# Expert sums of a decoder layer: v rows gathered for each token, against one dense pass over the v table for two tiles at a time

## The reference, cut to what matters

```
q = (xb @ wq).reshape(tokens, 8 heads, 2, 128)
s = einsum('thpd,pkd->thpk', q, subkeys)          # two lists of 128 scores for each head
s1, i1 = top_k(s[:, :, 0], 16);  s2, i2 = top_k(s[:, :, 1], 16)
top_s, sel = top_k(s1[..., :, None] + s2[..., None, :], 16)   # 16 of 256 pairs
idx = (i1 * 128 + i2)[sel]                        # one of 16384 experts
g   = softmax(top_s)
act = gelu(einsum('thkd,td->thk', u_tab[idx], xb))
y   = einsum('thk,thkd->td', g * act, v_tab[idx])
```

## Time and profile before

| | us |
|---|---|
| runs | 2040.8, 2052.54, 2053.34 |
| median | 2052.54 |
| profiled execution, first to last instruction | 2046.0 |
| TensorE busy (share) | 1616.0 (79%) |
| VectorE busy | 1207.7 (59%) |
| ScalarE busy | 476.3 (23%) |
| GpSimd busy | 1134.0 (55%) |
| bytes moved | 713 MB, 349 GB/s over the span |
| of these by GpSimd's queue (the gathers) | 570 MB |

### The profile page before, as it was taken

The page is one execution under the profiler, slowest core; times in us unless marked ns, Lnnn a source line. Parts: engine busy times, 40 slices in busy tenths (PEclk is TensorE's granted clock), DMA queues, the critical chain, the costliest instruction groups (busy, mean ns, idle before and its releaser), DMA issues.

```text
span 2046.0 us, 20838 instructions
## 1 busy us (share of the span) xinstructions
PE 1616.0 (79%) x5461; PEld 764.0 (37%) x5461; DVE 1207.7 (59%) x3129; ACT 476.3 (23%) x1217; POOL 1134.0 (55%) x1168
## 2 busy tenths in 40 slices
PE   6979989983767457768888888788878789599966
PEld 1524546451126113223433344333433344255422
DVE  2222355867766701116767766677667689679972
ACT  1221313130101021212223222222222223223321
POOL 3000021322873555777777667767777677577773
PEclk8989999996775679998999989899999899899988
DMA  8795676896995599999999999999999999799995
GB/s 319 254 364 207 215 263 218 305 337 135 355 385 179 198 401 404 392 416 394 400 420 420 400 368 418 419 373 420 420 401 391 388 403 419 308 412 417 414 372 226
DMA packets 237575, 713.43 MB, mean 349 GB/s; under 512 B 23102, under 2 KB 49056, under 8 KB 237457
## 3 DMA queue, kind: packets, MB, share of 16 engines
q0 software_dynamic: 156672, 570.49, 71.2%
q1 hardware_dynamic: 80488, 140.73, 19.4%
q10 hardware_dynamic: 312, 1.07, 0.2%
HBM read 704.42 MB, written 8.25 MB: 348 GB/s over the span
## 4 chain that ended last, share of the span: by engine, by line
PE 19%; DMA 14%; DVE 12%; issue 7%; POOL 7%; ACT 5%; DVEq 0%; POOLq 0%; ACTq 0%
PE ps_y L2316 13%; DVE u_rows L2095 6%; DMA v_rows<-in_peer_v_dram,expert_idx_ring 5%; DMA v_rows<-in_peer_v_dram,tile_idx 5%; PE ps_r L2290 4%; POOL u_rows L1890 3%; DMA u_rows<-in_peer_u_dram,expert_idx_ring 3%; POOL v_rows L1896 2%; POOL v_rows L1904 2%; ACT wt_diag L1987 2%; PE ps_y L2331 2%; DMA v_rows<-in_peer_v_dram,sample_idx 1%; DVE key_scores_w L2106 1%; ACT L2002 1%; ACT L2033 1%
## 5 line engine op out<-in xcount | busy, mean ns | idle before, releaser
L2316 PE MATMUL ps_y<-v_rows,wt_diag 128*128 128x512 f32 x1664 | 796.9, 621 | 146.6 <-DMA v_rows<-in_peer_v_dram,expert_idx_ring 65.2
L2316 PEld LDWEIGHTS ps_y<-v_rows,wt_diag 128*128 128x128 f32 x1664 | 311.4, 197 | 571.1 <-issue 547.5
L1890 POOL DMA_INDIRECT u_rows<-in_peer_u_dram,expert_idx_ring x384 | 368.2, 959 | 164.7 <-issue 90.3
L2095 DVE CUSTOM_DVE_ANT_0 u_rows<-u_rows,ps_y 128x1024 f32<-128x1024 f32 x360 | 420.4, 1218 | 64.1 <-DMA u_rows<-in_peer_u_dram,expert_idx_ring 58.1
L1896 POOL DMA_INDIRECT v_rows<-in_peer_v_dram,expert_idx_ring x384 | 366.7, 955 | 120.2 <-issue 99.3
L341 POOL DMA_INDIRECT low_rows<-in_peer_u_dram,tile_idx x128 | 174.7, 1364 | 214.7 <-DVE tile_dots L333 148.5
L607 PE MATMUL ps_z<-w_stream,hT 128*128 128x512 f32 (+5 forms) x560 | 249.0, 602 | 36.9 <-DMA w_stream<-in_w_in_dram 19.7
L2331 PE MATMUL ps_y<-v_rows,wt_diag 64*64 64x512 f32 x1024 | 135.1, 645 | 57.4 <-DMA v_rows<-in_peer_v_dram,tile_idx 50.8
L333 DVE CUSTOM_DVE_ANT_0 low_rows<-low_rows,tile_rows 128x1024 f32<-128x1024 f32 x128 | 152.9, 1232 | 44.1 <-DMA low_rows<-in_peer_u_dram,tile_idx 31.9
L607 PEld LDWEIGHTS ps_z<-w_stream,hT 128*128 128x128 f32 (+1 forms) x560 | 100.9, 185 | 163.9 <-issue 132.6
L1904 POOL DMA_INDIRECT v_rows<-in_peer_v_dram,tile_idx x128 | 122.1, 954 | 71.8 <-PE ps_y L2331 44.6
(11 more groups left out here) (434 smaller groups left out, 1628.3 us busy)
## 6 DMA issues: line engine op xcount, KB each, us to landing
w_stream<-in_w_in_dram SPq DMA_DIRECT2D x25, 2048.0 KB, 12.8
w_stream<-in_ada_w_dram SPq DMA_DIRECT2D x12, 2048.0 KB, 12.8
w_stream<-in_peer_wq_dram SPq DMA_DIRECT2D x8, 1024.0 KB, 8.5
wq<-in_peer_wq_dram SPq DMA_DIRECT2D x4, 2048.0 KB, 42.2
w_stream<-in_w_in_dram SPq DMA_DIRECT2D x5, 1568.0 KB, 8.5
w_stream<-in_w_in_dram SPq DMA_DIRECT2D x5, 1536.0 KB, 17.5
u_rows<-in_peer_u_dram,expert_idx_ring POOLq DMA_INDIRECT x384, 7.4
v_rows<-in_peer_v_dram,expert_idx_ring POOLq DMA_INDIRECT x384, 7.9
```

Of the source, the lines that this page charges most:

```text
L1890: g.indirect_dma_start(u_rows[:, j, :], None, U, bass.IndirectOffsetOnAxis(where[:, j:j + 1], 0))\
L2095: v.tensor_tensor_reduce(u_rows[:, j, :], u_rows[:, j, :], row[:, :], 1.0, 0.0, ALU.mult, ALU.add, dots[:, par, j:j + 1]).then_inc(s["u_us ...
L2316: mm = nc.tensor.matmul(ps_y[:, c * 512:(c + 1) * 512], diag[:, par, j, :], v_rows[:, j, c * 512:(c + 1) * 512], start=(first and j == 0), ...
```

## The change

Routing is taken out of the loop over groups. q is made for all 416 remaining tokens at once, head by head; the scores of a head go to DRAM (`sc_dram`) and come back tile by tile. The work is then a list of 26 head steps `G`: 8 for each of tiles 2 to 4, and 2 for the samples, each with 16 u gathers and 16 dots.

The v gathers stay for tile 1 alone: 40 of them up front, the other 88 one to one with the u gathers of the first head steps. Its sums are now full 128x128 products. For tiles 2 to 4 and the samples the weights of all experts become dense matrices. Expert (a, b) is row a*128 + b of the table. For each token, VectorE compares the 128 selected a and b with 0..127 (`compare`), ScalarE scales one of the two one-hot matrices by the weights (`weigh`), and TensorE multiplies them (`build`), which gives the 128x128 matrix W of that token. Four tokens make a group; 32 groups a tile, 8 for the samples. W of two tiles fills the 16 MB of `expert_weights`.

Then the v table is streamed twice in 128 slabs of 128 rows (all a, one b), which SP loads with plain DMAs into rings: pass 1 serves tiles 2 and 3, pass 2 tile 4 and the samples (four slabs at a time, in four groups of 32 columns). W of tile 4 is built during the last 38 slabs of pass 1, that of the samples between the passes. The finish of tiles 1 to 3 is done in pass 2.

```
+DOT_GROUPS = {}
+for _n in range(TILE_GROUPS):
+    DOT_GROUPS.setdefault((NH - PH - 5) * TOPK + 2 * _n + 1, []).append(_n)
+    DOT_GROUPS.setdefault(2 * PH * TOPK + 6 + _n, []).append(TILE_GROUPS + _n)
+    DOT_GROUPS.setdefault(3 * PH * TOPK + 6 + _n, []).append(2 * TILE_GROUPS + _n)
...
 sync:
+                for n in range(2 * PK):
+                    dst, landed, _ = slab(n)
+                    m = n - PK
+                    if m < 0:
+                        if n >= 4:
+                            sp.wait_ge(s["passed"], n - 3)
+                    elif m < 4:
+                        sp.wait_ge(s["passed"], PK - 3 + m)
+                    elif m < 8:
+                        sp.wait_ge(s["u_used"], SLOTS)
+                    else:
+                        sp.wait_ge(s["passed"], PK + (m - 8) // 4 * 4 + 4)
+                    sp.dma_start(dst, I["peer_v"][0].rearrange("(a b) d -> a b d", b=PK)[:, n % PK, :]).then_inc(landed, 16)
 gpsimd:
+                def v0_gather(k):
+                    j = k % NB
+                    if k >= NB:
+                        pool.wait_ge(s["v_used"], k + 1 - NB)
+                    g.indirect_dma_start(v0_rows[:, j, :], None, V, ...)
...
+                for G in range(HEADS):
+                    pool.wait_ge(s["routed"], G + 1)
+                    if PH <= G + 2 < HEADS:
+                        load_scores(G + 2)
...
+                    first = V0_EARLY * NB + G * TOPK
+                    for r in range(TOPK):
+                        u_gather(G, r)
+                        if first + r < P:
+                            v0_gather(first + r)
 scalar:
+                def weigh(T, n):
+                    act.wait_ge(s["oh_cmp"], n + 1)
+                    for t in range(TG):
+                        col = (n - W_BASE[T]) * TG + t
+                        last = a(onehot[:, n % 2, 1, t, :], onehot[:, n % 2, 1, t, :], ACT.Copy, scale=tT[:, 0, col:col + 1])
+                    last.then_inc(s["oh_w"], 1)
 vector:
+                def compare(n):
+                    T = max(t for t in W_BASE if W_BASE[t] <= n)
+                    dve.wait_ge(s["w_out"], BANK_BASE[T] + 1)
+                    if n >= 2:
+                        dve.wait_ge(s["w_full"], bank_use(n - 2) + 1)
+                    t0 = (n - W_BASE[T]) * TG
+                    v.tensor_tensor(onehot[:, n % 2], iota[:, :].unsqueeze(1).unsqueeze(1).broadcast_to([P, 2, TG, PK]),
+                                    repeat_last(tT[:, 1:3, t0:t0 + TG], PK), ALU.is_equal).then_inc(s["oh_cmp"], 1)
...
+                for G in range(HEADS):
...
+                    for r in range(TOPK):
+                        take_dot(G, r)
+                        if r == 3 and G + 2 < HEADS:
+                            keys(G + 2)
+                        if r == 11 and G + 2 < HEADS:
+                            pairs(G + 2)
...
+                        for n in DOT_GROUPS.get(G * TOPK + r, ()):
+                            compare(n)
 tensor:
+                for h in range(PH):
+                    pe.wait_ge(wq_in[h // 2], 16)
+                    head(h)
+                    sums0(2 + h)
+                for i in range(2 + PH, TOPK):
+                    sums0(i)
+                columns_t(1)
+                for n in range(TILE_GROUPS):
+                    build(n)
+                columns_t(2)
+                for n in range(TILE_GROUPS, 2 * TILE_GROUPS):
+                    build(n)
+                pe.wait_ge(s["w_out"], BANK_BASE[2] + 1 + TILE_GROUPS)
+                pe.wait_ge(s["y_out"], 1)
+                for i2 in range(PK):
+                    products(i2, W[1][:, i2, :], 1)
+                    products(i2, W[2][:, i2, :], 2).then_inc(s["passed"], 1)
+                    if i2 == W3_FROM - 1:
+                        columns_t(3)
+                    if W3_FROM <= i2 < W3_FROM + TILE_GROUPS:
+                        build(2 * TILE_GROUPS + i2 - W3_FROM)
+                columns_t(ST)
+                for n in range(96, 96 + W_COUNT[ST]):
+                    build(n)
+                pe.wait_ge(s["w_out"], BANK_BASE[ST])
+                for i2 in range(PK):
+                    mm = products(PK + i2, region[:, i2 // HALF, i2 % HALF, :], 3)
+                    if i2 % 4 == 3:
...
+                        for c in range(2):
+                            for q in range(4):
+                                b = i2 - 3 + q
+                                mm = nc.tensor.matmul(y_banks[ST][c][q * NS:(q + 1) * NS, :], W[ST][:, b, :], ...)
+                        mm.then_inc(s["passed"], 4)
```

More of the change, by code:

```diff
@@ L2075, in _ @@
-                for k in range(2, GPT + 1):
-                    slot((LT - 1) * GPT + k, k % 2, pairs=LAST_PAIRS.get(k), keys=LAST_KEYS.get(k),
-                         squares=(LT, NS) if k == LAST_ROWS - 1 else None, rows=LT if k == LAST_ROWS else None)
-                y_copy(NG - 1)
-                group(NG + 1, 1)
-                root(NT - 1)
-                group(NG + 2, 0)
-                group(NG + 3, 1)
-                y_copy(NG + SG - 1)
-                root(NT, NS)
+                a(subT, bank[0][:, 0:2 * PK].rearrange("p (k n) -> p k n", k=2), ACT.Copy).then_inc(s["subT_out"], 1)
@@ L2182, in slot @@
-                def slot(i, par, gates, pairs=None, keys=None, before=None, rows=(h_ps, h_ps)):
-                    weigh(i, par, gates)
-                    if pairs is not None:
-                        route_pairs(*pairs)
-                    if before:
-                        before()
-                    take_dots(i + 1, 1 - par, range(0, NB // 2), rows[0])
-                    if keys is not None:
-                        route_keys(keys)
-                    take_dots(i + 1, 1 - par, range(NB // 2, NB), rows[1])
@@ L2194, in pair @@
-                def pair(i, first, H, p, before=None, rows=(h_ps, h_ps)):
-                    slot(i, 0, gate[:, bass.ds(first, NB)], keys=H, rows=rows)
-                    slot(i + 1, 1, gate[:, bass.ds(first + NB, NB)], pairs=(H, p + 2), before=before, rows=rows)
-                def finish(t, n, src, row):
-                    hold(dve, s["x1_in"], t * 16 + 16)
-                    chain(v.tensor_tensor(y[0:n, :], src, row, ALU.mult))
-                    chain(v.tensor_tensor(x1[0:n, :], x1[0:n, :], y[0:n, :], ALU.add))
-                    v.tensor_tensor_reduce(y[0:n, :], x1[0:n, :], x1[0:n, :], 1.0, 0.0, ALU.mult, ALU.add, fs[0:n, 0:1])\
-                        .then_inc(s["ss_ready"], 1)
-                    hold(dve, s["rt_ready"], t + 1)
+                    spread = iota[:, 0:TOPK].unsqueeze(1).unsqueeze(1).broadcast_to([P, 2, TOPK, TOPK])
@@ new lines, in finish @@
+                def finish(t, n, halves, row):
+                    dve.wait_ge(s["x1_in"], 16 * (NT + 2))
+                    x, y = x1[t][0:n, :], tmp[t % 2][0:n, :]
+                    for c, half in enumerate(halves):
+                        last = v.tensor_tensor(y[:, c * 512:(c + 1) * 512], half[0:n, :], row[0:n, c * 512:(c + 1) * 512], ALU.mult)
+                    chain(last)
+                    chain(v.tensor_tensor(x, x, y, ALU.add))
+                    v.tensor_tensor_reduce(y, x, x, 1.0, 0.0, ALU.mult, ALU.add, fs[0:n, 0:1]).then_inc(s["ss_ready"], 1)
+                    dve.wait_ge(s["rt_ready"], t + 1)
@@ L2244, in _ @@
-                chain.base, chain.n = outer + (LT - 1) * TILE, 0
-                def last_head(k):
-                    H = LAST_PAIRS.get(k)
-                    return None if H is None else (H, H if H < LT * PH else None)
-                def sample_norm():
-                    gained(NS, gain_s, 2 + 2 * B, 2)
-                    norm(LT, NS)
-                for k in range(2, GPT):
-                    first = (LT - 1) * P + k * NB
-                    last = k == GPT - 1
-                    if last:
-                        dve.wait_ge(s["hs_in"], 16 * QS)
-                        dve.wait_ge(spread_in[0], 2 * 16 * QS)
-                    slot((LT - 1) * GPT + k, k % 2, gate[:, first:first + NB], pairs=last_head(k), keys=LAST_KEYS.get(k),
-                         before=sample_norm if k == LAST_ROWS - 1 else None, rows=(h_smp, h_smp) if last else (h_ps, h_ps))
@@ L2277, in _, with sums0 @@
                 e = K["ident"]
-                def rows_t(t):
-                    hold(pe, s["h_normed"], t + 1)
+                def sums0(i):
+                    for j in range(NB):
+                        pe.wait_ge(s["diag_ready"], i * NB + j + 1)
+                        pe.wait_ge(v_in[j], i * 16 + 16)
+                        for c in range(2):
+                            mm = nc.tensor.matmul(bank[c][:, :], diag[:, i % 2, j, :], v0_rows[:, j, c * 512:(c + 1) * 512],
+                                                  start=(i == 0 and j == 0), stop=(i == TOPK - 1 and j == NB - 1))
+                        mm.then_inc(s["v_used"], 1)
```

877 lines of the change are left out of this document (436 added, 441 removed).

## The result

The changed kernel takes 2366.9 us (median of 4 runs, 2363.9 to 2374.0). The kernel before takes 2050.9 us on the same chip (4 runs, 2040.8 to 2053.3). The ratio is 1.155, with a 95% interval of 1.151 to 1.159: 316 us slower. The forecast was 2405 us, 353 us slower. The profiled execution took 2363.9 us and its span is 2362.2 us; against that span stands the sum of 2402.

A forecast was written before the change was run, and what follows sets the result against it. The prediction took DMA (1228 us of gathers) and GpSimd (1190 us) to bound the kernel before. The change's serial stages, added in order, gave 2402 us, 2408 against the run median, stated as 2405; range 2325 to 2520.

The forecast's parts named there:

- Step 1: From the start to the first routed head: head 0 at 781 us, routed at 816, first dot at 846.
- Step 2: Tile 2's u dots during tile 1's sums: 8 u gathers per 29 us, later 2.49 us a pair; sums end near 1130.
- Step 3: From 1141 us VectorE is the bound, 27.4 us a head without compares; W of tile 3 ready at about 1567.
- Step 4: First pass over the v slabs: 439 us of products, 46 builds, 2 waits, 20 for fighting gathers; end at 2074.
- Contention: In the first pass, slabs and gathers ask for 458 GB/s against 420, slowing some 35 slabs; taken as 20 us.
- Builds: In the first pass's last 38 slabs, 32 builds of four 128x128 products at 0.36 us each: 46 us.
- Step 5: Builds for the samples between the passes: 8 at ScalarE's 1.9 us plus 6 us to fill, 21 us, to 2095.
- Step 6: Second pass: 219 us of slab products plus 64 us of 32-column products on four column groups, 284 us, to 2379.
- the rival with 155 us more: In the second pass the 32-column products do not overlap: 219 us instead of 64, total 2560; chance 5%.
- the late slabs: In the second pass four slabs land together, every second group waits 3.9 us: 62 us, total 2467; chance 13%.
- Step 7: After the second pass: 11 us as before, plus 5 us for tile 4's finish ahead of the samples', to 2395.
- Step 8: TensorE's granted clock in the passes: 1% of 723 us, 7 us; at 0.94 it would be 45.

The follow-up runs named there:

- Experiment 2: The changed kernel with all eight heads made ahead of tile 1's sums 2 to 15: 2331.2 us, ratio 1.140 to the kernel before.
- Experiment 3: The changed kernel with each dot over 512 of the 1024 columns, gathers whole: 2285.3 us, one run.
- experiment 5: The changed kernel with both passes multiplying only columns 0 to 511 of each slab, slabs loaded whole: 2138.8 us, one run.
- Experiment 7: The changed kernel with the v table streamed three times, tile 2's pass starting once its own W is whole: 2395.2 us, ratio 1.166 to the kernel before.

## Why the prediction came true, step by step

In each step the measured time stands first.

- **Step 1, start.** First dot 840.8, predicted 846. The order of head, scores to DRAM and back, keys and pairs was worked from rows and each held.
- **Step 2, tile 2's dots.** Period 28.96 us against 29, tile 1's sums end at 1130 against 1130. Experiment 2 shows that the heads hold the u gathers, and that without the heads between the sums the DMA limit binds there; the gain is 35 us.
- **Step 3, VectorE.** From 1141 to 1564 it was busy 98%; first product at 1564.8 against 1567. GpSimd waits for dots in this stretch and not the other way round (its table of waits, 1141 to 1564, first row: who waited, for whom, us, times, longest). Experiment 3 shows it as cause: 79 us for half of the dots' columns.

```profile
POOL u_rows L1940 <- DVE tile_dots L2241: 103.2, 84, 6.9
```

- **Step 4, first pass.** 468.7 us against 507. The prediction had 439 + 46 + 2 + 20; the trace has 128 slabs of 3.44 us (440) and 28.5 of builds, with no waits. Two terms were mis-sized. **Contention** was put at 20 us and is 0: from 1564 to 1745 TensorE is busy 180.31 of 181 us at a DMA share of 1.02. The fight falls on the gathers: VectorE waits 25.2 us for u rows, and nothing on the chain waits for those dots. The row taken for it, the wq load at 4.3 us for 0.524 MB, was of another kind. Bytes by queue of the kernel before, 717 to 785 us, where q1 carries wq (packets, MB, share of the 16 engines):

```profile
q0 software_dynamic: 4570, 16.67, 60.4%
q1 hardware_dynamic: 5101, 10.96, 42.4%
```

  Of q1's 10.96 MB only 8.4 are wq; the rest is other loads of SP. So the queue as a whole moved 161 GB/s, where the prediction read 123, and 161 is already more than the 153 that the slabs ask for: read by queue, this row gives no contention. The packets are near even, but q1's hold 2.1 KB and the gathers' 3.6 KB, so q1 got 40% of the bytes. A slab's packets are as large as a gather's (3.6 KB in experiment 5), and there its even share is 205 GB/s. The Trainium skill (DMA: Bandwidth & Descriptors, "Queues, rings and completion order") says that each DMA engine goes round the queues that have work, a packet at a time. Its packet is a group of some 9 to 17 descriptors, while the profile counts 144 packets to a gather of 128 rows, so the turns themselves are not seen here. The near-even counts agree with the rule, and by it the term would have been 0. **Builds** were put at 46 us (0.36 us a 128x128 product) and took 28.5 (0.89 a build of four, which is 8 records). The row of 0.71 us for four records holds the latency of the last record, and in a run each record adds 0.11 us. A length in the timeline is no period; starts of neighbours are.
- **Step 5, sample builds.** 2033.5 to 2052.7, 19 us against 21.
- **Step 6, second pass.** 285.4 us against 284: four slabs in 7.06 + 1.85 = 8.92 us, 32 times. The 32-column products overlap on four column groups as the row had it; the rival with 155 us more fell, and so did the late slabs. A slab lands 5.0 us (median) after its issue (the page's DMA issues: count, KB each, us), and no product of either pass waited for one.

```profile
v_ring<-in_peer_v_dram SPq DMA_DIRECT2D x192, 512.0 KB, 5.0
```

- **Step 7, tail.** 24 us against 16, the one step that was too short. The wait behind tile 4's finish was in the sum, at 5 us, and took 4.1. The fold of the samples, at a granted clock of 0.50, took 1.7 us more than before. The other 7 us lie behind the last store, which had been 2.3 us ahead of the end and is now 9.3. What changed there is that GpSimd issues it and not SP, and the change's code has that line; no run moved the store back, so the cause is open. The eight experiments, which keep that line, have the same 9.3 us.
- **Step 8, clock.** 0 us against 7. Granted were 1.00 in every window of both passes. The 0.94 to 0.96 of the earlier trace rows belonged to stages with gaps.
- **Work at no cost.** VectorE's waits from 1141 to 2050, first row:

```profile
DVE pair_onehots L2224 <- ACT pair_columns L2055: 148.3, 2, 119.7
```

  It stood 119.7 us in one piece before the first compare for tile 4, and no engine on the chain waited for it.

In order (start of the first pass, first pass, sample builds, second pass, tail, clock) the forecast was too long by 2.2, 38.3, 1.8, -1.4, -8.1 and 7 us: together 39.8, the whole difference between 2402 and 2362.2.

The sum came out closer than its parts: the start was within about 5 us at every point, and the first pass was 38 us too long, of which the tail gave 8 back. One sign that the prediction named came out only in part: TensorE was not "nearly idle" from 1141 to 1564 but 30% busy with builds, at a granted clock of 0.50 to 0.62.

What makes it 15% slower is thus not one wait but the order: 773 us of TensorE's work (469 + 19 + 285) cannot begin before VectorE has finished two tiles, while before the change products, dots and gathers of one group ran beside the next. Experiment 5 measures the one side (half the products: 228 us less), experiment 3 the other (half the dots' columns: 82 us less), and neither alone, nor the traffic saved, reaches the old time. Both halves in one kernel were not run. Experiment 7 starts TensorE 121 us earlier and loses it again to the DMA engines, so an earlier start alone is not enough either. Not tried was a mixture, v gathers for tile 2 as before and dense passes only for the others, which would give TensorE work during VectorE's stretch.

## What to carry to other kernels

Taking away 77 MB from a kernel at its DMA limit is worth nothing if the work that remains can no longer run side by side: before costing the bytes, write down for each engine when its first and last instruction of the new scheme can run, and add along the chain. Where two queues share the DMA engines, ask how much each one wants: here the one that wanted less than half (152 of 406 GB/s) was served in full and the other paid. And read the price of an instruction from the starts of its neighbours in a long run, not from the length of a short one.

## What was not expected of the hardware

- Two queues that both want more get about as many packets each, whether those come from an indirect gather or a plain load: 1127 and 1126 in 20 us, 5654 and 5599 in 100 us, 4570 and 5101 in 68 us. With packets of one size that is an even split of the bytes (20.39 and 20.22 MB), with 2.1 against 3.6 KB it was 40 to 60. A queue that asked for 152 GB/s moved 153, with the other at 252 (25.21 MB in 100 us).
- Rows 512 KB apart load as fast as neighbouring rows: 184.1 and 184.2 us for the second pass, 359 GB/s in the same window.
- A 128x128 float32 record in a run of long products costs 0.11 us, a quarter of the 0.43 of a 128x512 record: between these two the cost goes by columns.
- The same four 32-column records (the samples' fold) took 1.92 us at a granted clock of 1.00 and 3.63 us at 0.50.
- A last store of 128 KB issued by SP was followed by the end of the execution after 2.3 us, one issued by GpSimd after 9.3 us. One pair of kernels, not isolated.
